# A triangular inverse inside a gated delta rule: 32 by 32 diagonal blocks side by side on TensorE, then two levels of sub-blocks

## The chip, the cores and the metric

One core of one Trainium2 chip runs the whole program once. The metric is the device time of one execution in microseconds. Before the change the median of three runs is 1224.68 us (1224.17 to 1226.65).

## What is computed

Two layers over one sequence of 512 tokens, width 1024, in fp32. The first block (banded attention, pooling, a gated feed-forward part) is not touched. The second is a hybrid mixer of four heads: a gated delta rule, which needs the solution of a unit lower triangular system per chunk, and a differential attention, both on projections of the normed input. The part of the reference that matters:

```python
def gated_delta_rule_chunked(q, k, v, g, beta):
    ...
    decay = jnp.exp(jnp.where(tril, g[..., :, None] - g[..., None, :], -jnp.inf))
    lower = jnp.where(strict, jnp.einsum("bhncd,bhnmd->bhncm", k_beta, k) * decay, 0.0)
    a_mat = lower + jnp.eye(c, dtype=q.dtype)
    rhs = jnp.concatenate([v_beta, k_beta * jnp.exp(g)[..., None]], axis=-1)
    sol = lax.linalg.triangular_solve(a_mat, rhs, left_side=True, lower=True, unit_diagonal=True)
    u, w = sol[..., :dv], sol[..., dv:]
    qk_intra = jnp.where(tril, jnp.einsum("bhncd,bhnmd->bhncm", q, k) * decay, 0.0)
    # then a scan over the chunks that carries a 128 x 128 state
```

## The kernel before

Channels lie on the 128 partitions and tokens along the free dimension. The kernel takes the delta rule in chunks of 128 tokens (four, `NT`), where the reference has 64, which is the same sum in another order. All dense products are made in units: 128 output channels, 8 steps (`KT`), each step three products of 128x128 weights with 512 columns (a high and a low part of both operands), L481, L482 and L484. Per unit ScalarE rounds the weights (L1550), VectorE makes their low part (L944), SyncE loads them in a ring of four.

The second block runs in four stages (`STAGES`, L446). Stage `a` has the `dense` work of head `a` (z, K, Q, v of the attention, and c0 to c2, the convolution inputs, of the next head), the preparation `prep` of head `a` for the delta rule, and for head `a - 1` the `scan` over the chunks and the attention `diff`. Stage 0 has no `scan` and no `diff`, the last stage no c units. Within a stage each engine's program order is made by `Rounds`: the chains (`scan`, `diff`, `pair_norms`, `prep`) are generators, in one round each of them runs to its next `yield`, and then `dense` advances by a number of filler steps, PACE_SCORES while `diff` makes scores and PACE_PREP (or PACE_FIRST in stage 0) after that. All five engines count the same rounds, so the order on each is fixed when the program is built, and only semaphores tie them together. Once `dense` is empty, rounds hold chain work alone. After the four stages, at about 1154 us, follow the last head's `scan` and `diff` with the output projection between.

In `prep`, TensorE's part (L711) computes L^T for the four chunks of a head into `LT` (512 columns). The inverse is then made by doubling: `Ti` and `TiT` hold the inverse of the diagonal blocks of 2^lv and its transpose. For each level 1 to 6 the product `y` (L755, by `per_tile`, L708) multiplies the off-diagonal blocks, cut out of `LT` by GpSimd with a mask into `LmT` (L1961), with `Ti`; ScalarE copies it from PSUM bank 6 into `Y` (L1760); `t` (L762, L765) multiplies by `TiT` on both sides into bank 7, and VectorE subtracts the result from `Ti` and `TiT` (L1292, L1294). Level 0 is a mask and a subtraction (L1276, L1281), for which TensorE turns L once (`turn_tiles`, L703). All products are fp32, 128x128 weights per chunk, and each is two records in the trace. In level 1 `kt` and `qk` are made as well, once `scan` of the head before is over. At the end `u` and `w` (L780, L781) multiply with `TiT`, ScalarE and VectorE copy them (L1773, L1315), and the next stage's `scan` begins with L809.

`pair_norms` sums the squares of Q and K over each head half (L794), once the Q unit's products are issued (`qk_round`); its bank is the one that the scores of `diff` use. `Qb` and `Kr` are single buffers: ScalarE writes those of head `a` (L1849) after the scores of head `a - 1`. Other lines named below: L728 sums squares over partitions for `rqk` (16 records that stream one column), L835 spreads the norms of K over two column halves of the array, L862 makes scores on 64 partitions, one row half of the array for each of two banks, L808 and L476 are waits of TensorE's sequencer (`scan`'s, and a unit's).

## Time and profile before

| | |
|---|---|
| median of 3 runs | 1224.68 us |
| profiled execution | 1226.45 us |
| span of its instructions | 1225.0 us |
| granted TensorE clock, mean | 0.965 of 2.4 GHz |
| second block, stages 0 to 3 | about 787 to 1154 us |

The profile is of one execution. PE is TensorE's products, PEld its weight loads, DVE VectorE, ACT ScalarE, POOL GpSimd. A row of the timeline joins neighbouring instructions of a line: its start, the time from the first's start to the last's end, their number after the x, and in brackets the idle time before it with what ended it. The ends of products are modelled, so a group's cost to TensorE is read from start to start: from its start to that of what follows.

### The profile page before, as it was taken

What the parts mean: (1) busy time and instruction counts of PE and PEld (TensorE: products, weight loads), DVE (VectorE), ACT (ScalarE), POOL (GpSimd) and SP (SyncE); (2) the same over time, 40 slices, a digit from 0 to 9 for tenths busy, and PEclk for the clock granted to TensorE, in tenths of its full rate; (3) what the DMA queues carried; (4) which work ended last, traced back from release to release, by engine and by line L of the source; (5) the groups of instructions that cost most, each with busy time, mean ns of one, the idle gap of its engine ahead of it and who ended that gap; (6) DMA issues with size and microseconds to landing.
All of it is one profiled execution on the core that took longest, in us unless ns stands there. A gap on an engine that the chain in (4) does not pass through costs nothing.

```text
span 1225.0 us, 14195 instructions
## 1 busy us (share of the span) xinstructions
PE 1148.6 (94%) x5632; PEld 929.9 (76%) x5632; DVE 654.4 (53%) x1071; ACT 447.0 (36%) x742; POOL 128.9 (11%) x106
## 2 busy tenths in 40 slices
PE   6999999999989999999999996989899899899798
PEld 5777878788768888888888875678778678678676
DVE  5544444546337888777732227545383574474274
ACT  5232323244443544444432223332442453253232
POOL 1000000000110000000000001022233133033110
PEclk9999999999989999999999997989899999999699
DMA  8122222212321333332323331211011111111001
GB/s 331 52 70 69 69 69 70 69 52 86 103 86 52 102 105 104 104 103 89 101 86 104 104 103 57 76 52 37 33 35 52 52 35 52 36 50 37 18 18 69
DMA packets 25313, 91.63 MB, mean 75 GB/s; under 512 B 2848, under 2 KB 3104, under 8 KB 25120
## 3 DMA queue, kind: packets, MB, share of 16 engines
q1 hardware_dynamic: 23040, 83.90, 20.9%
q0 software_dynamic: 768, 4.53, 0.9%
q10 hardware_dynamic: 1440, 2.31, 0.5%
q8 instruction: 45, 0.74, 0.3%
q14 instruction: 20, 0.16, 0.0%
HBM read 88.63 MB, written 2.10 MB: 74 GB/s over the span
## 4 chain that ended last, share of the span: by engine, by line
PE 82%; DVE 10%; ACT 4%; issue 3%; POOL 1%; DMA 0%; ACTq 0%; DVEq 0%
PE PS L481 19%; PE PS L484 18%; PE PS L482 18%; PE PS L708 4%; PE PS L574 2%; DVE Wl L944 2%; PE PS L765 2%; ACT Wh L1550 1%; PE PS L596 1%; PE PS L762 1%; PE PS L915 1%; PE PS L917 1%; PE PS L916 1%; PE PS L509 1%; PE PS L510 1%
## 5 line engine op out<-in xcount | busy, mean ns | idle before, releaser
L481 PE MATMUL PS<-Hh,Wh 128*128 128x512 f32 x856 | 355.1, 415 | 2.1 <-DVE Hl L1126 2.1
L484 PE MATMUL PS<-Hh,Wl 128*128 128x512 f32 x856 | 338.0, 395 | 0.0
L482 PE MATMUL PS<-Hl,Wh 128*128 128x512 f32 x856 | 337.1, 394 | 0.0
L944 DVE TENSOR_TENSOR Wl<-raw,Wh 128x1024 fp32r<-128x1024 f32 x156 | 192.2, 1238 | 194.5 <-ACT Wh L1550 193.2
L481 PEld LDWEIGHTS PS<-Hh,Wh 128*128 128x128 f32 x856 | 163.3, 191 | 48.4 <-issue 16.1
L484 PEld LDWEIGHTS PS<-Hh,Wl 128*128 128x128 f32 x856 | 162.7, 190 | 36.1
L1550 ACT ACTIVATE Wh<-raw 128x1024 fp32r<-128x1024 f32 x156 | 162.3, 1050 | 67.8 <-PE PS L484 48.2
L482 PEld LDWEIGHTS PS<-Hl,Wh 128*128 128x128 f32 x856 | 163.7, 191 | 29.2 <-issue 0.7
L481 PE MATMUL PS<-Ah,Wh 128*128 128x512 f32 x176 | 69.8, 396 | 0.0
L482 PE MATMUL PS<-Al,Wh 128*128 128x512 f32 x176 | 69.8, 396 | 0.0
L484 PE MATMUL PS<-Ah,Wl 128*128 128x512 f32 x176 | 69.8, 396 | 0.0
L1592 ACT ACTIVATE sq<-sq,nmax 128x512 f32<-128x512 f32 (+3 forms) x32 | 18.0, 563 | 106.8 <-DVE nmax L1056 106.8
L1923 POOL MEMSET ssum<- 128x512 f32 x2 | 1.1, 528 | 509.2 <-DVE Hl L1126 282.3
L1961 POOL TENSOR_TENSOR head_LmT<-head_LT,mats 128x512 f32<-128x512 f32 x28 | 37.5, 1340 | 134.9 <-PE PS L708 102.7
L509 PE MATMUL PS<-Hh,Wh 128*128 128x512 f32 x72 | 32.4, 450 | 18.3 <-DVE Hl L958 18.3
L1760 ACT ACTIVATE head_Y<-PS 128x512 f32<-128x512 f32 x24 | 14.3, 596 | 82.6 <-PE PS L708 82.6
L1653 ACT ACTIVATE sq<-PS 128x512 f32<-128x512 f32 x16 | 9.6, 598 | 91.5 <-PE PS L484 91.5
L983 DVE TENSOR_TENSOR tmp<-PS,RB 128x512 f32<-128x512 f32 x44 | 30.3, 691 | 21.2 <-PE PS L484 19.0
L1681 ACT ACTIVATE conv<-conv 128x512 f32<-128x512 f32 x22 | 13.9, 633 | 71.0 <-DVE conv L1141 71.0
L484 PEld LDWEIGHTS PS<-Ah,Wl 128*128 128x128 f32 x176 | 33.1, 188 | 8.1
L482 PEld LDWEIGHTS PS<-Al,Wh 128*128 128x128 f32 x176 | 33.1, 188 | 8.1
L481 PEld LDWEIGHTS PS<-Ah,Wh 128*128 128x128 f32 x176 | 33.1, 188 | 8.1
(290 smaller groups left out, 1741.6 us busy)
## 6 DMA issues: line engine op xcount, KB each, us to landing
raw<-in_w_units SPq DMA_DIRECT2D x156, 512.0 KB, 3.5
X<-in_x SPq DMA_DIRECT2D x4, 512.0 KB, 6.8
relb<-in_rel POOLq DMA_DIRECT2D x1, 2048.0 KB, 10.2
out<-X ACTq DMA_DIRECT2D x8, 256.0 KB, 2.0
mats<-in_mats POOLq DMA_DIRECT2D x1, 832.0 KB, 4.7
window<-in_window POOLq DMA_DIRECT2D x1, 544.0 KB, 13.0
rope<-in_rope POOLq DMA_DIRECT2D x1, 512.0 KB, 5.2
wgrp<-in_wgrp POOLq DMA_DIRECT2D x1, 256.0 KB, 10.9
```

The source lines that it names most:

```text
L481: pe.matmul(bank, Wh[:, s, w], rhs[0](r), start=first and j == 0, stop=False)
L482: pe.matmul(bank, Wh[:, s, w], rhs[1](r), start=False, stop=False)
L484: ins = pe.matmul(bank, Wl[:, s, w], rhs[0](r), start=False, stop=last and end)
L509: pe.matmul(banks[u], Wh[:, s, w], Hh[:, k, :], start=k == 0, stop=False)
L574: pe.matmul(PS[:, 2 + b % 2, 0:nk], Q2[r, tok(qt)], K2[r, 0:nk], start=True, stop=True).then_inc(*att_pe.tick(i, ("scores", b)))
L708: ins = pe.matmul(bank[:, tok(t)], lhs[:, tok(t)], rhs[:, tok(t)], start=True, stop=True)
L765: ins = pe.matmul(b7[:, 2 * P + t * H:2 * P + (t + 1) * H], Y[:, tok(t)], blocks(TiT[:, tok(t)], size, 1), start=True, stop=True)
L944: dv.tensor_tensor(Wl[:, s, :], raw[:, s, :], Wh[:, s, :].bitcast(F32), sub).then_inc(unit_split, 1)
L983: return dv.tensor_tensor(dst, PS[:, bank_of[g], :], RB[:], mult).then_inc(bank_read[g % 2], 1)
L1550: ac.activation(Wh[:, s, :], raw[:, s, :], ACT.Copy).then_inc(unit_rounded, 1)
L1592: ac.activation(w, w, ACT.Exp, bias=nmax[:, b:b + 1], scale=1.0, accum_out=rsum[:, b:b + 1]).then_inc(*att_ac.tick(i, ("exp", b)))
L1961: gp.tensor_tensor(tiles(LmT[:]), tiles(LT[:]), over_tiles(mat(K_LEVEL + 1 + lv)), mult).then_inc(*prep_gp.tick(i, ("lm", lv)))
```

## The change

The diagonal blocks of 32 by 32 are inverted first (levels 1 to 4), the blocks of all four chunks side by side: `LTc`, `TcT`, `Tc` and `Yc_` are 128 x 128 each, four strips of 32 partitions, each strip with its block of the four chunks. `inverse_y` and `inverse_t` multiply block by block, 16 products of 32 x 32 a half-level, each on the array tile of its strip. Only `TcT` is updated, and VectorE's transpose, which turns 32 by 32 blocks, makes `Tc` from it. Level 5 joins blocks of 32 to 64 (8 and 12 products) and level 6 blocks of 64 to 128 (4 and 4). The masks of levels 1 to 4 are one VectorE operation (`lm`) in place of GpSimd's one per level; two operations each of VectorE and ScalarE gather the strips. GpSimd zeroes `TiT` and `T64` once. A level takes three rounds instead of four, `prep` in all ten fewer. The paces get values of their own per stage, `pair_norms` waits until scoring is over, and Q and K of the attention have two buffers each.

The diff, cut to its core (the semaphores' step lists, the mask constants on the host and the renamed operands of `diff` are left out):

```diff
+BLK, N_LEVELS = 32, 7
+N_MATS = K_LEVEL + 2
...
-PACE_SCALARS, PACE_SCORES, PACE_PREP, PACE_END, PACE_FIRST = 3, 1.3, 1.9, 1.5, 1.5
+PACE_SCALARS, PACE_END = 3, 1.5
+PACE_SCORES, PACE_PREP = (None, 1.9, 1.9, 1.25), (1.75, 2.3, 2.3, 1.25)
...
-    Qb, Kr, Vd, Vdt, Od, Wd = (
-        sb("head_" + n, [P, S]) for n in ("Qb", "Kr", "Vd", "Vdt", "Od", "Wd"))
-    Bm = Lm = Y
+    Vd, Vdt, Od, Wd = (sb("head_" + n, [P, S]) for n in ("Vd", "Vdt", "Od", "Wd"))
+    Qs, Ks = (sb("heads_" + n, [P, 2, S]) for n in ("Qb", "Kr"))
+    Bm = Y
     Kb = Lo
+    LTc, TcT, Tc, Yc_ = (Ti[:, n * P:(n + 1) * P].rearrange("p (t n) -> p t n", t=NT) for n in range(4))
+    T64 = sb("T64", [P, NT, 2 * BLK])
+    Y6 = Y[:, 0:NT * 2 * BLK].rearrange("p (t n) -> p t n", t=NT)
...
+    def strip(n):
+        return slice(n * BLK, (n + 1) * BLK)
+    def diagonal(ap, n):
+        return tiles(ap)[strip(n), :, strip(n)]
...
-            st.scanning = b is not None
+            st.scanning = st.scoring = b is not None
...
-            while b is not None and not st.scores_done:
-                st(PACE_SCORES)
+            while st.scoring:
+                st(PACE_SCORES[a])
             while st.dense:
-                st(PACE_PREP if b is not None else PACE_FIRST)
+                st(PACE_PREP[a])
...
+        def inverse_y(lv):
+            for t in range(NT):
+                own = slice(t * BLK, (t + 1) * BLK)
+                if lv < 5:
+                    for n in range(P // BLK):
+                        ins = pe.matmul(b6[strip(n), own], LmT[strip(n), P * (lv - 1) + t * BLK:
+                                                               P * (lv - 1) + (t + 1) * BLK],
+                                        Tc[strip(n), t, :], start=True, stop=True)
+                elif lv == 5:
+                    for n in (0, 2):
+                        ins = pe.matmul(b6[strip(n + 1), own], tiles(LT[:])[strip(n), t, strip(n + 1)],
+                                        Tc[strip(n), t, :], start=True, stop=True)
+                else:
+                    ins = pe.matmul(b6[P // 2:, 2 * t * BLK:2 * (t + 1) * BLK],
+                                    tiles(LT[:])[0:P // 2, t, P // 2:], T64[0:P // 2, t, :],
+                                    start=True, stop=True)
+            return ins
+        def inverse_t(lv):
+            for t in range(NT):
+                own = slice(t * BLK, (t + 1) * BLK)
+                if lv < 5:
+                    for n in range(P // BLK):
+                        ins = pe.matmul(b7[strip(n), own], Yc_[strip(n), t, :], TcT[strip(n), t, :],
+                                        start=True, stop=True)
+                elif lv == 5:
+                    for n in (0, 2):
+                        pe.matmul(b7[strip(n), own], Yc_[strip(n + 1), t, :], TcT[strip(n + 1), t, :],
+                                  start=True, stop=True)
+                    ins = pe.matmul(b7[strip(1), own], TcT[strip(1), t, :], Yc_[strip(1), t, :],
+                                    start=True, stop=True)
+                else:
+                    ins = pe.matmul(b7[0:P // 2, 2 * t * BLK:2 * (t + 1) * BLK], Y6[P // 2:, t, :],
+                                    tiles(TiT[:])[P // 2:, t, P // 2:], start=True, stop=True)
+            return ins
...
-            pe.wait_ge(*prep_dv.at(i, "lt"))
-            turn_tiles(b6, LT).then_inc(*prep_pe.tick(i, "turned"))
-            yield
-            yield
-            yield
             yield
             for lv in levels:
-                size = 1 << lv
-                pe.wait_ge(*prep_gp.at(i, ("lm", lv)))
-                pe.wait_ge(*prep_dv.at(i, ("t", lv - 1) if lv > 1 else "ti"))
-                per_tile(b6, LmT, Ti).then_inc(*prep_pe.tick(i, ("y", lv)))
-                yield
+                pe.wait_ge(*prep_dv.at(i, ("t", lv - 1) if lv > 1 else "lm"))
+                if lv == 1:
+                    pe.wait_ge(*prep_ac.at(i, "strips"))
+                if lv == 2:
+                    pe.wait_ge(*prep_dv.at(i, "at"))
+                if lv == 6:
+                    pe.wait_ge(*prep_ac.at(i, "wide"))
+                inverse_y(lv).then_inc(*prep_pe.tick(i, ("y", lv)))
                 yield
                 pe.wait_ge(*prep_ac.at(i, ("y", lv)))
-                H = P // 2
-                if lv + 1 < N_LEVELS:
-                    for t in range(NT):
-                        pe.matmul(b7[:, t * H:(t + 1) * H], TiT[:, tok(t)],
-                                  blocks(Y[:, tok(t)], size, 0), start=True, stop=True)
-                for t in range(NT):
-                    ins = pe.matmul(b7[:, 2 * P + t * H:2 * P + (t + 1) * H], Y[:, tok(t)],
-                                    blocks(TiT[:, tok(t)], size, 1), start=True, stop=True)
-                ins.then_inc(*prep_pe.tick(i, ("t", lv)))
-                yield
+                inverse_t(lv).then_inc(*prep_pe.tick(i, ("t", lv)))
                 yield
                 if lv == 1:
                     while st.scanning:
@@ -774,8 +818,7 @@
                     pe.wait_ge(*prep_dv.at(i, ("t", lv)))
                     per_tile(b7, CK, CQ).then_inc(*prep_pe.tick(i, "qk"))
                     yield
-                    yield
-                    pe.wait_ge(*prep_dv.at(i, "at"))
+                yield
...
-            while st.qk_round is None:
+            while st.qk_round is None or st.scoring:
...
-            yield
-            dv.wait_ge(*prep_gp.at(i, ("lm", 0)))
-            dv.tensor_tensor(tiles(TiT[:]), over_tiles(ident[:]), tiles(LmT[:]),
+            dv.wait_ge(*prep_dv.at(i, "lt"))
+            dv.tensor_copy(LTc[strip(0)], diagonal(LT[:], 0))
+            dv.tensor_copy(LTc[strip(1)], diagonal(LT[:], 1)).then_inc(*prep_dv.tick(i, "strips"))
+            yield
+            dv.wait_ge(*prep_dv.at(i, "strips"))
+            dv.wait_ge(*prep_ac.at(i, "strips"))
+            if i:
+                dv.wait_ge(*prep_ac.at(i - 1, "wide"))
+            dv.tensor_tensor(TcT, LTc, over_chunks(mat(K_LEVEL + 1)[:, 0:BLK]),
+                             mult).then_inc(*prep_dv.tick(i, "m0"))
+            dv.wait_ge(*prep_dv.at(i, "m0"))
+            dv.tensor_tensor(TcT, over_chunks(mat(K_LEVEL + 1)[:, BLK:2 * BLK]), TcT,
                              sub).then_inc(*prep_dv.tick(i, "tt"))
-            yield
-            yield
-            dv.wait_ge(*prep_gp.at(i, "l0"))
-            dv.tensor_tensor(tiles(Ti[:]), over_tiles(ident[:]), tiles(Lm[:]),
-                             sub).then_inc(*prep_dv.tick(i, "ti"))
+            dv.wait_ge(*prep_dv.at(i, "tt"))
+            dv.transpose(flat(Tc), flat(TcT)).then_inc(*prep_dv.tick(i, "ti"))
+            dv.tensor_tensor(
+                LmT[:].rearrange("p (l t n) -> p l t n", l=4, t=NT),
+                LTc.unsqueeze(1).to_broadcast([P, 4, NT, BLK]),
+                mat(K_LEVEL).rearrange("p (l n) -> p l n", l=4).unsqueeze(2).to_broadcast(
+                    [P, 4, NT, BLK]), mult).then_inc(*prep_dv.tick(i, "lm"))
             yield
             for lv in levels:
-                size = 1 << lv
-                yield
-                yield
                 yield
                 dv.wait_ge(*prep_pe.at(i, ("t", lv)))
-                if lv + 1 < N_LEVELS:
-                    v = blocks(Ti[:], size, 0)
-                    dv.tensor_tensor(v, v, b7[:, 0:2 * P].rearrange("p (g b) -> p g b", b=size), sub)
-                v = blocks(TiT[:], size, 1)
-                dv.tensor_tensor(v, v, b7[:, 2 * P:].rearrange("p (g b) -> p g b", b=size),
-                                 sub).then_inc(*prep_dv.tick(i, ("t", lv)))
+                if lv < 5:
+                    dv.tensor_tensor(flat(TcT), flat(TcT), b7[:, 0:P],
+                                     sub).then_inc(*prep_dv.tick(i, ("tt", lv)))
+                    dv.wait_ge(*prep_dv.at(i, ("tt", lv)))
+                    dv.transpose(flat(Tc), flat(TcT)).then_inc(*prep_dv.tick(i, ("t", lv)))
+                    if lv == 4:
+                        dv.wait_ge(*prep_dv.at(i, ("t", lv)))
+                        dv.wait_ge(inverse_zeroed, 1)
+                        dv.tensor_copy(T64[strip(0), :, 0:BLK], Tc[strip(0)])
+                        dv.tensor_copy(T64[strip(1), :, BLK:],
+                                       Tc[strip(1)]).then_inc(*prep_dv.tick(i, "t64"))
+                elif lv == 5:
+                    z = b7[:, 0:P].rearrange("p (t n) -> p t n", t=NT)
+                    for n in (0, 2):
+                        dv.tensor_scalar(tiles(TiT[:])[strip(n), :, strip(n + 1)], z[strip(n)], -1.0,
+                                         None, mult)
+                    dv.tensor_scalar(T64[strip(1), :, 0:BLK], z[strip(1)], -1.0, None,
+                                     mult).then_inc(*prep_dv.tick(i, ("t", lv)))
+                else:
+                    z = b7[0:P // 2, 0:2 * P].rearrange("p (t n) -> p t n", t=NT)
+                    dv.tensor_scalar(tiles(TiT[:])[0:P // 2, :, P // 2:], z, -1.0, None,
+                                     mult).then_inc(*prep_dv.tick(i, ("t", lv)))
...
-            yield from idle(9)
-            ac.wait_ge(*prep_pe.at(i, "turned"))
-            ac.activation(Lo[:], b6, ACT.Copy).then_inc(*prep_ac.tick(i, "lo"))
-            yield
+            yield from idle(7)
+            ac.wait_ge(*prep_dv.at(i, "lt"))
+            ac.activation(LTc[strip(2)], diagonal(LT[:], 2), ACT.Copy)
+            ac.activation(LTc[strip(3)], diagonal(LT[:], 3),
+                          ACT.Copy).then_inc(*prep_ac.tick(i, "strips"))
             yield
             yield
             for lv in levels:
-                yield
                 ac.wait_ge(*prep_pe.at(i, ("y", lv)))
-                ac.activation(Y[:], b6, ACT.Copy).then_inc(*prep_ac.tick(i, ("y", lv)))
-                yield
+                if lv < 6:
+                    ins = ac.activation(flat(Yc_), b6[:, 0:P], ACT.Copy)
+                else:
+                    ins = ac.activation(flat(Y6)[P // 2:], b6[P // 2:, 0:2 * P], ACT.Copy)
+                ins.then_inc(*prep_ac.tick(i, ("y", lv)))
+                if lv == 5:
+                    ac.wait_ge(*prep_dv.at(i, ("tt", 4)))
+                    ac.wait_ge(inverse_zeroed, 1)
+                    for n in range(P // BLK):
+                        ins = ac.activation(diagonal(TiT[:], n), TcT[strip(n)], ACT.Copy)
+                    ins.then_inc(*prep_ac.tick(i, "wide"))
...
-                dst, j, c = (Qb, 0, C_QNORM) if name == "Qb" else (Kr, 1, C_KNORM)
+                dst, j, c = (Qs, 0, C_QNORM) if name == "Qb" else (Ks, 1, C_KNORM)
                 ac.wait_ge(*sum_read(g))
-                if a:
-                    ac.wait_ge(*diff_pe.at(a - 1, ("s", NT - 1, 1)))
+                if a > 1:
+                    ac.wait_ge(*diff_pe.at(a - 2, ("s", NT - 1, 1)))
                 ac.wait_ge(*prep_pe.at(a, "sums"))
-                ac.activation(dst[:], Yc[:, j, :], ACT.Copy, scale=col(c))
+                ac.activation(dst[:, a % 2, :], Yc[:, j, :], ACT.Copy, scale=col(c))
...
+        gp.memset(TiT[:], 0.0)
+        gp.memset(T64[:], 0.0).then_inc(inverse_zeroed, 1)
...
-            def level_mask(lv):
-                gp.tensor_tensor(tiles(LmT[:]), tiles(LT[:]), over_tiles(mat(K_LEVEL + 1 + lv)),
-                                 mult).then_inc(*prep_gp.tick(i, ("lm", lv)))
...
-            yield from idle(5)
-            gp.wait_ge(*prep_dv.at(i, "lt"))
...
-            yield
-            yield
-            for lv in levels:
-                yield
-                if lv + 1 < N_LEVELS:
-                    gp.wait_ge(*prep_pe.at(i, ("y", lv)))
-                    level_mask(lv + 1)
...
+            yield from idle(8)
+            while st.scanning:
+                yield
+            gp.wait_ge(*prep_pe.at(i, "qk"))
+            if i:
+                gp.wait_ge(*scan_pe.at(i - 1, ("o", NT - 1)))
+            gp.tensor_tensor(QG[:], CQ, EG[:], mult).then_inc(*prep_gp.tick(i, "qg"))
+            yield from idle(10)
```

## Rows read from the trace of the kernel before

**Rows 1.** Page, part 1: busy time, share of the span, instructions of each engine

```profile
...
PE 1148.6 (94%) x5632; PEld 929.9 (76%) x5632; DVE 654.4 (53%) x1071; ACT 447.0 (36%) x742; POOL 128.9 (11%) x106
...
```

**Rows 2.** Windows: us, PE, PEld, DVE, ACT, POOL busy; clock; DMA share; GB/s

```profile
...
871.00:967.00 96.00, 89.92 (x545) 75.35 (x545) 51.77 (x106) 36.65 (x73) 24.74 (x18) 0.97 0.14 45
...
1064.00:1154.00 90.00, 79.93 (x466) 67.29 (x465) 44.33 (x97) 33.91 (x69) 23.94 (x18) 0.88 0.09 30
...
1139.00:1160.00 21.00, 17.14 (x76) 14.83 (x77) 4.72 (x9) 5.60 (x7) 1.26 (x1) 0.51 0.00 1
...
```

**Rows 3.** Timeline, TensorE, one level, stage 0: start, us, instruction [idle before]

```profile
...
837.98 1.05 PE L708 MATMUL PS<-head_Ti,head_LmT 128*128 128x128 f32 x8
838.78 0.48 PE L481 MATMUL PS<-Hh,Wh 128*128 128x512 f32 x1
839.10 0.39 PE L482 MATMUL PS<-Hl,Wh 128*128 128x512 f32 x1
...
840.26 1.00 PE L762 MATMUL PS<-head_Y,head_TiT 128*128 128x64 f32 x8
841.10 1.06 PE L765 MATMUL PS<-head_TiT,head_Y 128*128 128x64 f32 x8
841.96 0.48 PE L481 MATMUL PS<-Hh,Wh 128*128 128x512 f32 x1
...
```

**Rows 4.** Timeline, TensorE: groups with small streams or part of the array

```profile
...
874.64 1.09 PE L835 MATMUL PS<-ident,rqk_b 128*64 128x128 f32 x16
875.66 1.12 PE L841 MATMUL PS<-head_Qb,mats 128*128 128x512 f32 x2
...
1080.56 0.39 PE L817 MATMUL PS<-head_VN,head_AT 128*128 128x128 f32 x2
1080.88 1.13 PE L862 MATMUL PS<-head_Kr,head_Qb 64*128 64x512 f32 x4
1081.93 0.50 PE L481 MATMUL PS<-Hh,Wh 128*128 128x512 f32 x1
...
1082.74 1.84 PE L728 MATMUL PS<-ones,sq 128*128 128x1 f32 x16
1084.44 0.48 PE L481 MATMUL PS<-Hh,Wh 128*128 128x512 f32 x1
...
```

**Rows 5.** Two lines, 874 to 875, sequencer: duration ns min/median/max, start us

```profile
...
L808 PEldq EVENT_SEMAPHORE  x1: 51/51/51, 874.1 to 874.1; - x1
...
L476 PEldq EVENT_SEMAPHORE  x1: 51/51/51, 874.7 to 874.7; - x1
...
```

**Rows 6.** Waits of TensorE, 785 to 1225: total us, times, longest us

```profile
...
PE PS L708 <- DVE head_TiT L1294: 9.0, 10, 2.1
PE PS L794 <- ACT sq L1850: 6.1, 4, 2.1
PE PS L809 <- DVE gs L1240: 6.1, 3, 2.6
...
PE PS L703 <- DVE rqk L1258: 3.5, 3, 1.2
PE PS L728 <- ACT sq L1749: 2.7, 1, 2.7
PE PS L762 <- ACT head_Y L1760: 2.6, 4, 0.7
...
```

**Rows 7.** Timeline, last stage, levels with nothing between

```profile
...
1141.56 1.97 PE L762 MATMUL PS<-head_Y,head_TiT 128*128 128x64 f32 x8 [0.69 <-ACT head_Y L1760]
...
1146.17 2.04 PE L708 MATMUL PS<-head_Ti,head_LmT 128*128 128x128 f32 x8 [0.94 <-DVE head_TiT L1294]
...
```

**Rows 8.** Three lines of VectorE: duration ns min/median/max, first and last start

```profile
...
L1276 DVE TENSOR_TENSOR head_TiT<-ident,head_LmT x4: 682/685/687, 821.7 to 1101.8; 128x512 f32<-128x512 f32 x4
...
L1337 DVE TENSOR_TENSOR head_VN<-head_U,PS x16: 273/280/289, 875.3 to 1184.0; 128x128 f32<-128x128 f32 x16
...
L1332 DVE MEMSET St<- x4: 165/165/165, 873.9 to 1155.9; 128x128 f32 x4
...
```

More of the change, by code:

```diff
@@ L349, in program @@
     levels = range(1, N_LEVELS)
[L350 removed]
+    prep_pe = steps("prep_tensor", ["g", "b", "sums", "vt", "kr", "kk", *(
         x for lv in levels for x in (("y", lv), ("t", lv), *(("kt", "qk") if lv == 1 else ()))), "u", "w"])
[L352 to L358 removed]
+    prep_dv = steps("prep_vector", ["gs", "d", "bm", "dt", "ms", "vb", "kn", "lt0", "lt", "strips",
+                                    "m0", "tt", "ti", "lm", *(
+        x for lv in levels for x in (*((("tt", lv),) if lv < 5 else ()), ("t", lv),
+                                     *(("t64",) if lv == 4 else ()),
+                                     *(("kd", "at", "rq") if lv == 1 else ()))), "wt"])
+    prep_ac = steps("prep_scalar", ["eg", "dt", "silu", "sq", "strips", *(
+        x for lv in levels for x in (("y", lv), *(("wide",) if lv == 5 else ()))), "u"])
+    prep_gp = steps("prep_gpsimd", ["rk", "rq", "qg"])
+    inverse_zeroed = semaphore("inverse_zeroed")
     pair_pe, pair_dv = steps("pair_norm_tensor", ["sums"]), steps("pair_norm_vector", ["ms", "q"])
@@ L398, in over_tiles, with over_chunks @@
         return ap.unsqueeze(1).to_broadcast([P, NT, P])
+    def over_chunks(ap):
+        return ap.unsqueeze(1).to_broadcast([P, NT, BLK])
     def over_cols(ap, n=P):
         return ap.unsqueeze(2).to_broadcast([P, ap.shape[1], n])
-    def blocks(ap, size, odd):
-        return ap.rearrange("p (g two b) -> p g two b", two=2, b=size)[:, :, odd, :]
+    def strip(n):
+        return slice(n * BLK, (n + 1) * BLK)
+    def diagonal(ap, n):
+        return tiles(ap)[strip(n), :, strip(n)]
     def flat(ap):
@@ L848, in diff @@
             pe.wait_ge(*diff_dv.at(i, "k"))
-            pe.matmul(s0, mat(K_SWAP), Kr[:], start=True, stop=True).then_inc(*diff_pe.tick(i, "ks"))
+            pe.matmul(s0, mat(K_SWAP), Ks[:, i % 2, :], start=True, stop=True).then_inc(*diff_pe.tick(i, "ks"))
             yield from idle(4)
@@ L879, in diff @@
                 yield
-            st.scores_done = True
+            st.scoring = False
             yield from out_norm(i, Od, 1, B_PT)
@@ L2037, in diff @@
             yield from idle(4 * (NT + 1))
-            st.scores_done = True
+            st.scoring = False
             yield from out_norm(i, 1)
@@ L2136, in _layout @@
             np.where(i <= j, 0.0, NEG), i < j]
-    for lv in range(N_LEVELS):
-        b = 1 << lv
-        low = (i // (2 * b) == j // (2 * b)) & (i // b > j // b)
-        mats += [low, low.T] if lv == 0 else [low.T]
+    c = t % BLK
+    r, c = np.meshgrid(c, c[:BLK], indexing="ij")
+    lows = [(r // (2 << lv) == c // (2 << lv)) & (c >> lv > r >> lv) for lv in range(5)]
+    mats += [np.concatenate(lows[1:], axis=1),
+             np.concatenate([lows[0], r == c, np.zeros((P, 2 * BLK))], axis=1)]
     mats = np.stack([m.astype(np.float32) for m in mats], axis=1)
```

55 lines of the change are left out of this document (13 added, 42 removed).

## The prediction

> **What bounds the kernel now.** I read the page's engine table first: TensorE is busy 94% of the span, VectorE 53% [rows 1]. So time can be won only where TensorE does less, stands idle less, or has more clock. Then the stretches: the change lies in the second block, whose four stages begin at about 787 us. A middle stage (871 to 967) has TensorE busy 89.9 of 96 us; the last one (1064 to 1154) 79.9 of 90 at a granted clock of 0.88; and from 1139 to 1160 the granted clock is 0.51, that is the 1.2 GHz level, with 17.1 of 21 us busy [rows 2]. Then TensorE's timeline for what one level of the inverse costs it [rows 3], and its waits for what ends its idle time [rows 6]. The other engines count only through these waits: GpSimd's level masks, 1.3 us each, end none of TensorE's idle time in those rows, so taking them away gives nothing by itself.
>
> **TensorE's work for the inverse, before.** In one level `y` holds TensorE from 837.98 to 838.78, 0.80 us, for 8 records, and `t` from 840.26 to 841.96, 1.70 us, for 16 [rows 3]. Every record costs about 0.105 us though `t` streams only 64 columns. The weights set this: 16 records that stream one column against 128 weight columns take 1.70 us, 0.106 us each [rows 4]. A head has five such levels, a last one with `y` and half of `t` (0.80 + 0.80) and the four turns of L (0.4): 12.5 + 1.6 + 0.4 = 14.5 us, 58 us for four heads at 2.4 GHz. The filler's first product after such a group starts its successor 0.1 us late (0.32 us instead of 0.23 [rows 3]); that stays and is not counted.
>
> **The same after.** Each fp32 product is two records. Levels 1 to 4 take 16 products in each half, 32 records; level 5 takes 8 and 12 products, 40 records: 4 x 64 + 40 = 296 records on tiles of 32 by 32 per head. Level 6 adds 16 records with 64 weight columns, at 0.106/2 = 0.053 us: 0.85 us. Nothing in the trace runs on a 32 by 32 tile, so a record's price c is bounded:
> - From above, one record after the other: a quarter of 0.106 for the weights and, as the stream costs 0.107 for 128 columns, 0.027 for the stream, 0.054 us together, nothing overlapping.
> - From below, two at a time: the 16 records of L835 on two column halves take 1.02 us up to the next start, though each streams 128 columns (0.107 us; 16 in a row would be 1.7) [rows 4]. The halves run side by side. The four records of L862 on two row halves do too: 1.05 us where four streams of 0.427 in a row would be 1.7 [rows 4]. Two of 0.027 side by side make 0.0135.
> - Between them, the sequencer: it passes L808 at 874.1 and L476 at 874.7, and decodes 24 pairs of weight load and product in these 0.6 us (2 + 16 + 2 + 4), 0.025 us a pair [rows 5]. The weight loads of consecutive records give 0.027.
> I take c = 0.030 us, next to these two. Going into and out of a tiled group also costs: L862 starts 0.1 us later after L817 than two records of 0.11 would have it, and L481 follows 0.2 us after its streams [rows 4]; I take 0.25 us a group, 12 groups a head. Sum per head 12 x 0.25 + 296 x 0.030 + 0.85 = 12.7 us, four heads 51 us, against 58: **-7.2 us**. The bounds of c give 4 x (3.85 + 16.0) = 79 (+21 us) and 4 x (3.85 + 4.0) = 31 (-27 us). So c decides the sign of this term.
>
> The row of L835 shows column tiles side by side. The Trainium skill, "TensorE: Matmul & The Clock Gate", Part 3, has tiles of different rows and columns run concurrently too, and in Part 1 a floor of about 25 ns from one small matmul's start to the next; that floor would make the sum 6 us smaller than mine (an estimate from that page), and the sequencer's pace agrees with it.
>
> **TensorE's idle time.** Program order here is made in rounds; each round lets every chain take one step and then runs filler steps. A filler step is three products, 0.69 us, and each ninth is empty. By the `yield`s in `prep` the chain took 46 rounds before and takes 36 after; `scan`, `diff` run in the first 27. Filler in a middle stage is 8 units of 9 steps = 72: before 27 x 1.3 = 35 and then 37/1.9 = 20 rounds, 47 in all; after 27 x 1.9 = 51 and 21/2.3 = 9, 36 in all. Both just cover the chain. The last stage has 45 steps: before they ended in round 33 and 13 rounds ran with nothing between; after, 27 x 1.25 and 11/1.25 = 9 give 36, none bare. Stage 0 (57 steps after the gate chain's 8 rounds): 38 of 46 rounds covered before, 33 of 36 after. What this does to the waits:
> - Waits inside the levels were 9.0 + 2.6 us by the rows and 2.8 more in two smaller groups of the same kind, 14.4 [rows 6]; 0.7 and 0.9 us each in the bare rounds [rows 7]. In the new order `y` to `t` is one round, 1.25 to 2.3 steps = 0.8 to 1.4 us, for ScalarE's copy, now a quarter as wide (0.60 before); `t` to `y` is two, 1.5 to 2.8 us, for a subtraction and a VectorE transpose. I price either by the 128x128 row, 0.28 us [rows 8]; the transpose has no row, bounds 0.17 (a memset of that size) and 0.69 (128x512); both fit under the cover. The start of the levels becomes dearer: VectorE alone does `lt0`, `lt`, two strips, `m0`, `tt`, the transpose and the 128x512 mask, about 0.69 x 3 + 0.28 x 4.5 = 3.3 us in a row, with what `scan`, `diff` and the weight splits queue before it (1.2 us each), under three rounds of 1.9 x 0.62 = 3.5 us and some of `diff`. I expect 1.7 us of new wait a head (0 to 3), 7 in all, and 2 elsewhere: 14.4 - 9 = **-5.4 us**.
> - The pair sums L794 wait 6.1 us, four times, for ScalarE's square of Q right behind it [rows 6]. With `pair_norms` held until scoring ends, and Q's unit over at step 36, which is round 19 of 27 in the middle stages, the square is long done there: 2 x 1.36 = **-2.7 us**. In the last stage step 36 comes at round 29, so the wait stays; so does stage 0's. The second buffer for Q and K takes a wait off ScalarE, which no row has on TensorE's path: nothing.
> - L703 waits 3.5 us in three stages for `rqk` [rows 6]; two rounds of 1.9 instead of 1.3 steps cover 0.75 us more, in two stages: **-1.5 us**. L728's 2.7 and L809's 6.1 (VectorE finishing the taps of the next head before the state's memset) have their mechanism unchanged: nothing.
> Together **-9.6 us** (-17 to -1).
>
> **Clock.** In the 21 us at 0.51 [rows 2] TensorE did 17.1 us of work that takes 8.6 at full clock; there groups of 8 records take 2.0 us instead of 1.0 [rows 7]. This stretch is the last stage's bare rounds and the weighty groups behind it. Filler between them should hold the 2.4 GHz level as in the middle stages (0.97 over 871 to 967); but the half-filled rounds are thinner (1.25 steps), and short stretches remain. I take **-5 us** of at most 8.5.
>
> **Sum.** 1226.45 (the profiled execution, 1.8 above the median of 1224.68) - 7.2 - 9.6 - 5 = 1204.6; less 1.8: 1203 us. The forecast's own range, c from 0.025 to 0.035 and the idle and clock terms at half their bounds, is 1192 to 1214.
>
> **Rivals.**
> - Row strips don't overlap (slower). All four strips write bank 6 or 7, where L862's row halves write two banks; L835, which shares a bank, has different columns only. If records go one by one, c = 0.054: 4 x 296 x 0.024 = 28 us more, 1231. It turns slower from c = 0.048. For it: no row has row strips in one bank. Against: their output partitions differ, as L835's do. The Trainium skill, "TensorEngine Tiling (Array Packing)", Restrictions and Gotchas, says different row tiles cannot access the same PSUM bank simultaneously; by that rule this rival holds, and no row here decides it.
> - The clock stays low where small products are thick: the last stage's ten-odd late rounds with their 15 us of filler at half pace. No gain of 5, and 8 us more: 1216. For it: the 0.51 stretch was made of small groups alone [rows 2, 7]. Against: the middle stages.
> - The idle time only moves: one round is too short for VectorE, whose queue holds splits and reads; the 9.6 us come back at the first level and in the last stage, 1213. This is also the case in which the new order doesn't do what it says.
> - Overlap better than I take it, c = 0.014 to 0.02: 1187 to 1191, 4 x 296 x 0.01 to 0.016 less.
>
> **How the numbers follow.** Forecast 0.50, strips one by one 0.13, low clock 0.14, idle moves 0.11, better overlap 0.12. A measurement of this kernel can tell 0.2% (2.4 us) from no change. Slower than 1227.1 is the first rival only: 0.13. Two rivals reach within 1222 to 1227 at their far ends: 0.06. Faster: 0.81. The range runs from the better overlap's 1187, less one, to 1226, and leaves out the slower rival and the lowest tail.
>
> **What would show it.** In the profile after: 32 records of a half-level within 1.0 to 1.4 us (one by one: 1.9); a wait of TensorE for VectorE's mask at the first level, 1 to 2 us a head; no wait of L794's successor in two stages; middle stages of about 91 us instead of 96; no half-clock stretch of 20 us before the output projection, and a last stage near 78 us instead of 89. A record above 0.05 us, or half-clock inside the filled rounds, would make the prediction wrong.

## The result, and the profile after

The changed kernel takes 1174.56 us (median of four runs, 1173.81 to 1176.38) against 1224.61 us: ratio 0.959, 95% interval 0.9574 to 0.9607. That is 50.1 us less, where 21.7 were forecast; the time lies below the forecast range of 1186 to 1226. The direction was right and the size was not. The two profiled executions, from which all rows come, have spans of 1225.0 and 1172.3 us, 52.7 us apart.

The page of the changed kernel, its first lines (span; busy time, share of the span and instructions of each engine):

```profile
span 1172.3 us, 15592 instructions
PE 1104.3 (94%) x6320; PEld 876.1 (75%) x6320; DVE 649.0 (55%) x1099; ACT 442.8 (38%) x762; POOL 87.1 (7%) x76
```

TensorE is still what bounds the kernel, at the same 94% as in [rows 1]; its work has shrunk with the span. The stages, by windows (columns as in [rows 2]), in the order 0, 1, 2, 3 and what follows the last stage:

```profile
791.90:859.90 68.00, 59.24 (x556) 47.20 (x555) 32.22 (x61) 21.34 (x34) 6.19 (x4) 0.90 0.15 47
859.90:945.60 85.70, 80.20 (x711) 62.29 (x711) 50.97 (x114) 34.62 (x77) 13.50 (x10) 0.98 0.16 50
945.60:1035.80 90.20, 84.74 (x710) 65.50 (x710) 52.84 (x116) 36.83 (x80) 13.53 (x10) 0.92 0.15 48
1035.80:1105.20 69.40, 63.24 (x639) 49.28 (x639) 42.69 (x101) 33.96 (x76) 14.82 (x10) 0.98 0.13 39
1105.20:1172.30 67.10, 60.38 (x302) 46.50 (x302) 42.13 (x83) 22.04 (x56) 7.97 (x6) 1.00 0.14 47
```

The same stretches of the kernel before, cut at the same lines, for comparison:

```profile
793.70:874.20 80.50, 69.54 (x384) 59.78 (x382) 34.27 (x54) 21.93 (x29) 16.73 (x12) 0.89 0.12 40
874.20:970.80 96.60, 88.93 (x539) 74.05 (x539) 52.51 (x107) 35.99 (x72) 24.74 (x18) 0.98 0.14 44
970.80:1067.30 96.50, 88.94 (x538) 73.62 (x539) 53.86 (x109) 38.11 (x75) 25.13 (x18) 0.98 0.14 44
1067.30:1156.20 88.90, 80.34 (x467) 67.89 (x467) 43.49 (x94) 34.33 (x70) 23.94 (x18) 0.87 0.09 30
```

All four stages gain, 12.5, 10.9, 6.3 and 19.5 us; what follows them is shorter by only 1.7 (68.8 before). In the first middle stage (the second line of both) TensorE's busy time fell by 8.7 of the 10.9 us at an equal clock of 0.98: work went away, more than waiting. The second middle stage has the same work but a granted clock of 0.92. The last had 0.87 and has 0.98.

What a half-level (the product `y` or `t` of one level) costs now, in TensorE's timeline of the changed kernel (start, time from first start to last end, tile and shape; levels 1, 1, 6 and 6; the trace calls `Tc` and `Yc_` by the name of their memory, `head_Ti`):

```profile
912.67 0.45 PE L733 MATMUL PS<-head_Ti,head_LmT 32*32 32x32 f32 x32
913.06 0.50 PE L497 MATMUL PS<-Hh,Wh 128*128 128x512 f32 x1
913.39 0.40 PE L498 MATMUL PS<-Hl,Wh 128*128 128x512 f32 x1
...
914.32 0.39 PE L500 MATMUL PS<-Hh,Wl 128*128 128x512 f32 x1
914.64 0.45 PE L752 MATMUL PS<-head_Ti 32*32 32x32 f32 x32
915.02 0.50 PE L497 MATMUL PS<-Hh,Wh 128*128 128x512 f32 x1
...
932.67 0.68 PE L741 MATMUL PS<-T,head_LT 64*64 64x64 f32 x8
933.28 0.50 PE L497 MATMUL PS<-Hh,Wh 128*128 128x512 f32 x1
...
934.86 0.67 PE L762 MATMUL PS<-head_TiT,head_Y 64*64 64x64 f32 x8
935.47 0.50 PE L497 MATMUL PS<-Hh,Wh 128*128 128x512 f32 x1
```

From start to next start 32 records take 0.39 and 0.38 us; half-levels of 8 and 16 records took 0.80 and 1.70 us before [rows 3]. The group of L733, seen alone:

```profile
L733 PE MATMUL PS<-head_Ti,head_LmT x32: 191/191/212, 912.7 to 912.9; 32*32 32x32 f32 x32
```

One record lasts 191 ns from start to end, but the first and the last of the 32 start only 0.26 us apart. In the single records of this group, four in a row, one on each strip, start 7 ns apart, and each four begins 32 ns after the start of the four before it (52 ns for the second four): 8 ns a record on the mean. Around the records lie 0.09 us ahead (the first starts 0.32 us after the filler's last product, where a filler product follows in 0.23) and 0.12 behind. The filler's first product after a group then starts its successor 0.1 us late, as in the kernel before (0.33 us here, 0.32 in [rows 3]).

TensorE's waits from 785 us on, after (line waiting, engine, tile and line waited for; us in total, times, longest):

```profile
PE PS L852 <- DVE gs L1283: 7.6, 3, 2.6
PE PS L837 <- ACT sq L1926: 4.8, 2, 2.8
PE PS L719 <- DVE head_Od L1427: 4.4, 2, 2.2
...
PE PS L733 <- DVE head_Ti L1344: 1.0, 1, 1.0
...
PE PS L756 <- ACT head_Ti L1827: 0.7, 1, 0.7
PE PS L733 <- DVE head_LmT L1331: 0.6, 1, 0.6
...
PE PS L724 <- DVE head_TiT L1360: 0.5, 1, 0.5
PE PS L752 <- ACT head_Ti L1827: 0.4, 1, 0.4
```

All of TensorE's waits above 0.15 us from 785 us on are 31.6 us in this execution and 40.9 in that of before.

The 52.7 us between the two executions can be split by the traces. From 785 us on, TensorE was busy 396.3 us before and 353.1 after; in 46.2 and 34.1 us of that the granted clock was at its 1.2 GHz level. If busy time at that level counts half, the work at 2.4 GHz is 373.2 and 336.0 us: 37 us less work, 6 us less lost to the clock, and the rest is idle time. The ends of products are modelled, and the run below with the old products has 371.3 us of work by the same count where it should have 373.2, so I take the work as known to some 2 us.

L852 is the old L809, L837 the old L794 and L719 the old L703 of [rows 6].

### The profile page after: what moved, and what is told of

The parts are those of the page before. It is cut to its first block, busy times and chain, and to the rows that moved or that the text cites. A ratio compares the mean times of both kernels' runs of the same rounds, so it can differ in the third digit from the quotient of the medians.

```text
span 1172.3 us, 15592 instructions
## 1 busy us (share of the span) xinstructions
PE 1104.3 (94%) x6320; PEld 876.1 (75%) x6320; DVE 649.0 (55%) x1099; ACT 442.8 (38%) x762; POOL 87.1 (7%) x76
## 4 chain that ended last, share of the span: by engine, by line
PE 82%; DVE 9%; ACT 5%; issue 3%; DMA 0%; POOL 0%; ACTq 0%; DVEq 0%
PE PS L497 20%; PE PS L500 19%; PE PS L498 19%; PE PS L590 2%; ACT Wh L1616 2%; PE PS L612 1%; PE PS L958 1%; PE PS L724 1%; PE PS L960 1%; PE PS L959 1%; DVE Wl L987 1%; PE PS L525 1%; PE PS L527 1%; PE PS L526 1%; PE PS L905 1%
## 5 line engine op out<-in xcount | busy, mean ns | idle before, releaser
L497 PEld LDWEIGHTS PS<-Hh,Wh 128*128 128x128 f32 x856 | 162.6, 190 | 50.2 <-issue 16.1
L1747 ACT ACTIVATE conv<-conv 128x512 f32<-128x512 f32 x22 | 13.9, 633 | 71.0 <-DVE conv L1184 71.0
L1734 ACT ACTIVATE conv<-tmp,cols 128x512 f32<-128x512 f32 x44 | 35.2, 802 | 7.3 <-DVE tmp L1026 7.3
L525 PEld LDWEIGHTS PS<-Hh,Wh 128*128 128x128 f32 x72 | 15.2, 211 | 25.0 <-issue 18.2
## 6 DMA issues: line engine op xcount, KB each, us to landing
wgrp<-in_wgrp POOLq DMA_DIRECT2D x1, 256.0 KB, 10.9
```

Source lines behind the costliest of these rows:

```text
L497: pe.matmul(bank, Wh[:, s, w], rhs[0](r), start=first and j == 0, stop=False)
L525: pe.matmul(banks[u], Wh[:, s, w], Hh[:, k, :], start=k == 0, stop=False)
L1734: ac.activation(conv[:, p % 2, j % 2, :], tmp[:, j % 2, :], ACT.Identity, bias=col(C_CONV + 4 * j + 3), scale=col(C_CONV + 4 * j + 2)).the ...
L1747: ac.activation(c, c, ACT.Gelu_apprx_tanh).then_inc(up_gelu, 1)
```

## The experiments

The theory: the products of the inverse became cheaper than forecast, because four strips run side by side at 8 ns a record, and the order of the work gave about what was forecast. The rival: the products gave the forecast 7 us, and the new order, with its thicker rounds, gave the rest through idle time and clock.

### The new products in the old order (against the kernel after)

```diff
-PACE_SCORES, PACE_PREP = (None, 1.9, 1.9, 1.25), (1.75, 2.3, 2.3, 1.25)
+PACE_SCORES, PACE_PREP = (None, 1.3, 1.3, 1.3), (1.5, 1.9, 1.9, 1.9)
 # PE, DVE, ACT: ahead of level 1
+            yield from idle(4)
 # PE, DVE, ACT: in each level, between y and t
+                yield
```

> The new products in the old order: the paces of the kernel before (1.5 in stage 0, then 1.3 and 1.9), one more round between y and t in each level and four more before the first level, so that prep takes 45 rounds again and the last stage has its bare rounds back; two buffers for Q and K stay. Theory A (of the 50 us some 40 are TensorE's work for the inverse and some 10 the order): about 1185 to 1190 us. Rival B (the order and the clock carry most, the products under 15): 1208 us or more.

Measured 1191.02 us against 1224.64, ratio 0.9721 (0.9695 to 0.9747). With as many rounds as before (46; the expectation is one short), the same number of filler steps in each, and a clock and waits close to those of before (0.964 beside 0.965, 41.0 us beside 40.9), 33.6 us are gone. It lies 1 us above the range that I gave. The second buffers and the holding back of `pair_norms` stay in, but the waits that the latter is aimed at are as before (6.7 us in four stages, 6.1 before), so they aren't part of the 33.6. By the split above this kernel has 336.2 us of work, as the kernel after has, and loses 2 us more to the clock than the kernel before: the work alone is some 36 to 37 us, a little more than the 33.6. The new order on top brings 16.5 us. So the rival falls: the larger part is the products. The last stage's bare rounds are back too, as this window of the kernel shows:

```profile
1110.00:1127.00 17.00, 12.83 (x107) 9.74 (x99) 5.84 (x14) 6.87 (x13) 1.16 (x1) 0.60 0.10 32
```

Thin small products with nothing between them, and a granted clock of 0.60, as in the stretch of [rows 2].

### The old products in the new order (against the kernel before)

```diff
-PACE_SCALARS, PACE_SCORES, PACE_PREP, PACE_END, PACE_FIRST = 3, 1.3, 1.9, 1.5, 1.5
+PACE_SCALARS, PACE_END = 3, 1.5
+PACE_SCORES, PACE_PREP = (None, 1.5, 1.5, 1.0), (1.25, 1.65, 1.65, 1.0)
...
-            while st.qk_round is None:
+            while st.qk_round is None or st.scoring:
```

> The kernel before with its own products and masks and its 46 rounds, but with the order's other parts: the pair sums held until scoring is over, and paces of each stage fitted so that filler lasts to the last round (1.25 in stage 0; 1.5 then 1.65 in the middle stages; 1.0 in the last, 1.3 then 1.9 before). It asks what the order is worth without the new products. Theory A (products carry most, and the order some 10 to 16 us only together with fewer rounds): 1212 to 1222 us. Rival B (spreading the filler and the clock carry most): 1200 us or less.

Measured 1215.19 us against 1226.08, ratio 0.9924 (0.9897 to 0.9951). The Q and K buffers stay single here, and the paces are spread over the 46 rounds of the old chain. An order made in the new manner brings 10.9 us by the medians without the new products (the interval allows 6 to 13). It is worth less than the 16.5 on top of them. Two things may be why: the old chain has 46 rounds to fill with the same work, and TensorE waits 5.4 us here for VectorE's scaling of `Oa`, a wait that the kernel before didn't have. No run takes the two apart.

### The loops over strips and chunks exchanged

```diff
+            if lv < 5:
+                for n in range(P // BLK):
+                    for t in range(NT):
+                        own = slice(t * BLK, (t + 1) * BLK)
+                        ins = pe.matmul(b6[strip(n), own], ...)
+                return ins
```

and the same in `inverse_t`.

> The changed kernel with the loops over chunks and strips exchanged in levels 1 to 4: the four chunks of one strip follow each other, so that eight records in a row lie on one 32 by 32 tile of the array. Nothing else differs. Theory A (the four strips work side by side, each taking one record per 32 ns; that is where the 0.39 us groups come from): the 1024 records of levels 1 to 4 cost 32 ns instead of 8, 24 us more, about 1199 us, and a group of 32 spreads over 1.0 us. Rival B (small records are cheap whatever their tile, and the strips need not be side by side): within 2 us of 1174.6.

Measured 1187.62 us against 1224.64, ratio 0.9691 (0.9668 to 0.9715): 13 us above the kernel after. The products and their number are the same; only which tile the next product goes to differs. TensorE's timeline:

```profile
912.53 0.89 PE L760 MATMUL PS<-head_Ti 32*32 32x32 f32 x32
913.36 0.50 PE L497 MATMUL PS<-Hh,Wh 128*128 128x512 f32 x1
```

0.83 us instead of 0.38 to 0.39, and 32 such groups make 14 us, which is the whole difference. Theory A had said 24 us more, and missed. The single records show why: they start 22.7 ns apart on the mean and not 32. Where records of one strip follow each other alone the gap is 31 to 32 ns, but nine of the 31 gaps are 5 or 6 ns, three for each change of strip, so records of two strips still overlap there. So alternating the strips is worth 13 to 14 us here, and even in this order a record costs less than the 30 ns that I took.

### Each group of levels 1 to 4 issued twice

```diff
+                if lv < 5:
+                    inverse_y(lv)
                 inverse_y(lv).then_inc(*prep_pe.tick(i, ("y", lv)))
...
+                if lv < 5:
+                    inverse_t(lv)
                 inverse_t(lv).then_inc(*prep_pe.tick(i, ("t", lv)))
```

> The changed kernel with every group of 32 records of levels 1 to 4 issued twice, into the same place in PSUM. It measures the price of a record without the way in and out of a group. Theory A: 1024 more records at 8 ns, 8 us, about 1183 us. At the 30 ns of the prediction it would be 31 us more, 1205 us. Rival B has no number of its own, since it puts the gain elsewhere.

Measured 1185.4 us, ratio 0.967 (0.9642 to 0.9699), 10.8 us above the kernel after:

```profile
897.04 0.75 PE L733 MATMUL PS<-head_Ti,head_LmT 32*32 32x32 f32 x64
897.72 0.50 PE L497 MATMUL PS<-Hh,Wh 128*128 128x512 f32 x1
```

0.68 us for 64 records, 0.30 more than for 32: 9.3 ns for one more record; by the time of the whole kernel, with 32 groups of 32 records added, 10.8/1024 = 10.5 ns (its interval allows 7 to 14). The starts of the 64 records are 8.9 ns apart on the mean. This is the price of a record without the way in and out, and it holds over twice as many records.

### A full product in the middle of each group

```diff
+                if lv < 5 and t == 2:
+                    pe.matmul(b6[:, 2 * P:3 * P], LT[:, 0:P], LT[:, 0:P], start=True, stop=True)
```

and the same into `b7` in `inverse_t`.

> The changed kernel with one product on the whole array (128 by 128 weights, 128 columns, two records, result unused) in the middle of each of the 32 groups of levels 1 to 4. It measures the way in and out of the tiled groups. The two records alone would cost 0.21 us, 6.8 us in all, 1181 us. Theory A, with 0.1 us to leave the tiles and 0.1 us to enter again: 0.41 us a group, 13 us, 1188 us. If the array had to run empty at each change for longer than the gap of 0.1 us seen before L862 in the kernel before, 1195 us or more.

Measured 1190.45 us, ratio 0.9717 (0.9691 to 0.9744), 15.9 us above the kernel after:

```profile
910.18 0.33 PE L735 MATMUL PS<-head_Ti,head_LmT 32*32 32x32 f32 x16
910.44 0.49 PE L732 MATMUL PS<-head_LT 128*128 128x128 f32 x2
910.85 0.33 PE L735 MATMUL PS<-head_Ti,head_LmT 32*32 32x32 f32 x16
911.11 0.50 PE L497 MATMUL PS<-Hh,Wh 128*128 128x512 f32 x1
```

The group takes 0.93 us instead of 0.39. Of the 0.54 more, the two records of the full product are 0.21 (0.105 each, as in [rows 3]) and 0.33 is for once more leaving the tiles and going back to them; by the time of the kernel it is 15.9/32 - 0.21 = 0.29. That is more than the 0.2 of theory A and more than the 0.21 us that I read around a group, but with the forecast's 0.25 the way in and out is of the right size.

### Three edits against the waits that are left

The kernel after has three waits with a cause in the order of work. Its timeline ahead of the L719 wait at 928.5:

```profile
925.17 1.25 ACT L1836 ACTIVATE head_TiT<-head_Ti 32x128 f32<-32x128 f32 x4
926.45 0.73 ACT L1916 ACTIVATE C<-Yc,cols 128x512 f32<-128x512 f32 x1
927.08 1.04 ACT L1616 ACTIVATE Wh<-raw 128x1024 fp32r<-128x1024 f32 x1
928.15 1.22 DVE L987 TENSOR_TENSOR Wl<-raw,Wh 128x1024 fp32r<-128x1024 f32 x1 [2.84 <-ACT Wh L1616]
929.29 0.74 DVE L1498 SCALAR_TENSOR_TENSOR C<-Yc,cols,C 128x511 f32<-128x511 f32 x1
929.95 0.68 DVE L1427 TENSOR_TENSOR head_Od<-head_Od,r_o 128x512 f32<-128x512 f32 x1
930.69 0.66 PE L719 MATMUL PS<-ident,head_Od 128*128 128x128 f32 x4 [2.19 <-DVE head_Od L1427]
```

ScalarE's four copies that widen `TcT` to `TiT` come all at once, 1.25 us, ahead of the rounding of the next weights; VectorE waits 2.84 us for it, then splits, makes a tap, and only then scales `Od`, for which TensorE has waited 2.19 us.

The first edit, the wide copies one round later:

```diff
                 ins.then_inc(*prep_ac.tick(i, ("y", lv)))
+                yield
                 if lv == 5:
...
                 yield
-                yield
```

> The changed kernel with ScalarE's four copies of the diagonal blocks (1.25 us, level 5) one round later. It is aimed at the new wait of 2.19 us of the turn of Od (L719) in both middle stages, and at the half-clock stretch of 10 us behind the second one. If the copies hold up ScalarE's rounding of the weights, VectorE's split behind it and so the scaling of Od, both waits go: 4 us, and up to 3 us more if the clock stays up: 1168 to 1171 us. If GpSimd's two powers (1.0 and 2.9 us, one behind the other since pair_norms is held) hold it up, nothing changes.

Measured 1167.48 us against 1226.08, ratio 0.9528 (0.9511 to 0.9545), just below the expected 1168 to 1171. What it tells of the clock is read from the second middle stage. The kernel after, behind its L719 wait, which ends at 1016.4, and the same place with the edit:

```profile
1017.00:1029.00 12.00, 12.00 (x45) 8.91 (x44) 5.82 (x9) 2.05 (x3) 0.00 (x0) 0.57 0.10 32
```

```profile
1012.00:1024.00 12.00, 10.91 (x68) 8.56 (x66) 8.32 (x14) 3.82 (x9) 0.01 (x1) 1.00 0.14 45
```

and two of the waits of the kernel with the edit:

```profile
PE PS L837 <- ACT sq L1926: 3.7, 2, 2.1
...
PE PS L719 <- DVE head_Od L1427: 2.2, 2, 1.1
```

Without the edit TensorE is busy for all of the 12 us, and for 10 of them at the 1.2 GHz level; with it the wait is 1.1 us, the clock stays at its 2.4 GHz level, and the two middle stages are of one length. The wait of L837 in the last stage falls by 1.1 us as well, since its square stood behind the same copies. By spans the edit gives 7.4 us, of which 3.3 are those waits. The rest, about 4, is near the 5 us that 10 us of busy time at half clock cost; no other stretch at the 1.2 GHz level came or went.

The second, the state's clearing moved from `scan` to behind the copy of `Wt` in `prep`, and in each round the chains before the taps:

```diff
-        for chains in (self.taps, self.chains):
+        for chains in (self.chains, self.taps):
...
             dv.tensor_copy(Wt[:], b7).then_inc(*prep_dv.tick(i, "wt"))
+            dv.memset(St[:], 0.0).then_inc(*scan_dv.tick(i, "start"))
```

> The changed kernel with two edits in VectorE's order: in each round its chains come before the convolution taps, and the scan's state is zeroed right behind the copy of Wt instead of in the next stage. It is aimed at the three waits of 2.5 us of L852 at the stages' borders. If these waits are VectorE's queue (a tap's chain of 0.7 to 2.3 us ahead of Wt and the memset), they fall to about 1 us and the time by 4 to 5 us, to 1170. If they are the copy of Wt itself behind the last products, 0 to 1 us.

Measured 1166.35 us, ratio 0.9514 (0.9491 to 0.9537). The 8.6 us that L852 waited (7.6 for `gs`, 1.0 for `St`) become 5.3, and L719's 4.4 become 3.1. That is more than the 4 to 5 us expected: all waits together fall by 5.1 us, the span by 5.4 and the median by 8.2.

The third, the pair sums of the last head three rounds later (`yield from idle(3)` ahead of them on all four engines where `i == GH - 1`):

> The changed kernel with the pair sums of the last stage three rounds later. It is aimed at the wait of 2.8 us of L837 for ScalarE's square of Q in the last stage. If only the distance to Q's unit sets it, the wait goes, 2.8 us, and with it perhaps the half-clock stretch of 3.4 us that follows (1.7 us): 1170 to 1172 us. If the sums then end the stage, the wait appears at the stage's border, and the time stays.

Measured 1168.83 us, ratio 0.9536 (0.9518 to 0.9554). L837's wait falls from 4.8 to 2.1 us; stage 0's is what stays. Expected were 1170 to 1172 us.

All three together:

> The changed kernel with the edits of the three runs before it together: VectorE's chains ahead of the taps and the state zeroed early, the wide copies a round later, the last pair sums three rounds later. If the waits they take away are apart in time, the gains add: 8.2 + 7.1 + 5.7 us off 1174.6 would be 1154 us. If they share a part (one late engine that delays the next in each of them), 1158 to 1162 us.

Measured 1159.16 us (1155.13 to 1159.86) against 1224.92, ratio 0.9453 (0.9435 to 0.9471). This is the fastest version but for the next, which can't be told from it: 15 us under the change. By spans the first, second and third edit alone give 7.4 + 5.4 + 3.2 = 16.0 us and the three 13.9, so about 2 us are shared. The waits say the same: they fall by 3.3, 5.1 and 2.9 us alone and by 9.3 together. Of the 2.0 shared, 1.1 is L837's wait, which the first and the third edit both shorten; L719's 2.2 and 1.3, from the first and the second, add up in full. On top of the three, the turn of `Od` one round later on TensorE and VectorE:

> As e11_three_edits, and the turn of Od (L719) and VectorE's product behind it one round later in the middle stages. What is left of that wait was 1.1 us a stage with the wide copies moved. If it is only a matter of distance, 2 us less than e11_three_edits; if the delay then meets the stage's border, no difference.

Measured 1158.62 us, ratio 0.9456 (0.9442 to 0.9471). The wait that it aims at was 0.9 us by then, and the time doesn't tell the two apart. The wait of the three edits together:

```profile
PE PS L719 <- DVE head_Od L1431: 0.9, 2, 0.4
```

Not tried: the second buffers for Q and K, and the holding back of `pair_norms`, each undone alone in the changed kernel. At its pace Q's unit is over before the scores are, and ScalarE, with one buffer, would wait for scores that stand in a later round. What each of the two brings stays open, as does what the ten fewer rounds bring without the new paces, and what fixes the 7 and 32 ns.

## Why the prediction was wrong

**TensorE's work for the inverse, forecast -7.2, measured -33.6 us.** This is the step that failed, in one term: c, the price of a record. Forecast 0.030 us; by the rows 0.26/32 = 0.008 in the groups of 32, and 0.009 over a head's 296 (level 5, which fills fewer strips, takes 0.25 and 0.26 us for 16 and 24). A head now costs 12 x 0.21 for the ways in and out, 2.6 for its 296 records, and 1.0 for level 6: 6.1 us, 24.4 for four heads against 58. Of the 26.6 us between this and the forecast 51, the records are 25, the ways in and out 2, and level 6 was 0.5 dearer than taken. The 0.1 us behind each group, which the 58 and the 24.4 both leave out, is the same before and after. So the rows give 33.6 us, the run with the old order 33.6, and the split of the busy time some 37; where the last 3 lie isn't shown. All of them pass even the forecast's lower bound of -27.

How c went astray is worth reading twice. The lower bound, 0.0135, is no bound: it took two streams side by side because L835 and L862 [rows 4] show two halves of the array, though four strips were about to be used; a fourth instead of a half of 0.027 is 0.007, where the runs found 0.008. And I drew c up to the sequencer's 0.025 us a pair [rows 5], which I read as a floor without a reason that excludes another limit behind it; the records of the changed kernel start 8 ns apart, and 64 of them in a row 8.9 ns. The Trainium skill, "TensorE: Matmul & The Clock Gate", Part 1, has about 25 ns as the least from start to start; across tiles of different strips no run here shows such a floor, and Part 3's picture of tiles side by side is what the trace has.

**The way in and out**, forecast 0.25 us a group: 0.21 by the rows, 0.29 to 0.33 for a leaving and a return by the experiment. Right.

**Idle time, forecast -9.6, by the traces -9.3 us.** The sum is right and its parts are only in part.
- The waits inside the levels and at their start fell from 14.4 to 3.2 us, where 9 were forecast, 7 of them new ones for the mask. That wait came once, with 0.6. I had put VectorE's way to it at 3.3 us against a cover of 3.5; the cover held. The subtraction and the transpose, which the forecast put at 0.28 us each, take 0.29 and 0.31.
- The waits for Q's squares went in the middle stages, as forecast, and stayed in stage 0 and the last; there the wait grew to 2.8, because the wide copies stand before the square. In sum 6.1 to 4.8 instead of 3.4.
- The 3.5 us for `rqk` are gone, 1.5 were forecast.
- Not forecast: 4.4 us for `Od`. The steps counted ScalarE's copies of `y` and left out the four wide ones, which only delay something two engines on. Also L852's waits grew from 7.1 us, with `St`, to 8.6.

**Clock, forecast -5 us.** The half-clock stretch of 20 us in the last stage [rows 2] is gone, and that stage's clock rose to 0.98. But a new one of 10 us came in the second middle stage, behind the wait for `Od`. From 785 us on the time at 1.2 GHz fell from 52 to 34 us. TensorE was busy in 46 and in all 34 of it, so the clock gives back half of 12, 6 us. Between the two executions waits and clock add up to 15 us; the run with the old order measures 16.5 for both, where the forecast had 14.6.

**The sum.** 1203 less 26.4 for the products (33.6 - 7.2) less 1.9 for order and clock (16.5 - 14.6) is 1174.7; measured 1174.56. It closes because both terms are taken from the same run; it shows only that the term of the products holds the error.

**The rivals.** Strips one by one (1231): refuted. The strips write one bank and start 7 ns apart, and even the kernel that goes strip by strip is 37 us faster than the one before, since its records take 23 ns and not 54. The Trainium skill, "TensorEngine Tiling (Array Packing)", Restrictions and Gotchas, keeps different row tiles out of one PSUM bank; tiles that differ in rows and columns, as these do, showed nothing of it. Low clock: it came in the second middle stage, for another reason than the one given, and small. Idle moves: 4.4 us for `Od` and 1.5 at L852 came anew, against 16 us of waits that went. The better overlap pointed the right way, but its c of 0.014 to 0.02 was cut off by the false bound. Its sum is also off at that end: 1203 less 4 x 296 x 0.016 is 1184 and not 1187, which would have put the range's lower end at 1183, still above the measured time.

**Signs named ahead.** 32 records in 1.0 to 1.4 us: 0.39. Mask wait of 1 to 2 us a head: no. No wait for the squares in two stages: yes. Middle stages of 91 us: 85.7 and 90.2. No stretch of 20 us at half clock: yes. Last stage of 78: 69.4.

## What to carry to other kernels

Price a product by the part of the array it takes: a quarter of the side in both directions, four at a time, costs here a thirteenth of a full record, if neighbours in program order go to different tiles; the order of two loops alone is worth 13 of the 34 us. Where no row shows an operation, a bound needs a reason why it can't be passed; a floor read from rows in which something else may be the limit is none, and one small measurement of a group would have been worth more than the rest of the sum. And a burst of small copies on an engine that shares the weights' preparation is to be followed two engines on: here 1.25 us of them cost 7 us by waits in three stages and the clock behind one of them.

## What the runs showed of the hardware

- fp32 products of 32 by 32 on four diagonal tiles start 7 ns apart, and each tile takes its next record 32 ns after the last (8 ns a record over 32). In a row on one tile alone they are 31 to 32 ns apart. One record lasts 191 ns from start to end, so those of the four tiles overlap, though all write one PSUM bank.
- Leaving the tiles for a full product and going back costs 0.33 us beyond the product by the timeline, 0.29 by the time of the kernel.
- After one wait of 2.19 us of TensorE the granted clock was at 1.2 GHz for 10 us, all of it busy (from 1017.8, 1.4 us after the wait's end); after the same wait of 2.19 us at 928.5, in the stage before, it stayed at its 2.4 GHz level (the window 929 to 941 has 1.00). The wait alone doesn't decide it; what does stays open.
